# First input tile of a two-block transformer kernel on unnormalised x, with the token scale put on at eviction

## What is computed

```python
u = rms_norm(h, attn_pre_norm[i])          # x * rsqrt(mean(x*x) + 1e-6) * gain, per token
c_q, c_kv, k_rope, m_q, m_k, m_v, m_o, m_i, m_f = split_cols(u @ w_in[i], IN_SIZES)
q = (rms_norm(c_q, q_norm[i]) @ w_uq[i])
kv = (rms_norm(c_kv, kv_norm[i]) @ w_ukv[i])
```

## Time and profile before

| what | value |
|---|---|
| time, median of 3 runs | 1800.66 us (1800.34 to 1800.88) |
| the profiled execution | 1801.43 us, span 1799.6 us |
| TensorE busy | 1786.2 us (99%), 8494 matmuls |
| VectorE busy | 1396.1 us (78%) |
| ScalarE busy | 698.4 us (39%) |
| GpSimd busy | 1101.1 us (61%) |
| granted TensorE clock, mean | 0.999 |
| chain that ended last | PE 78%, DVE 1% |

### The profile page before, as it was taken

One profiled execution on the slowest core, in us unless ns is written; L12 is line 12 of the kernel. 1 busy time (PEld: TensorE's weight loads), 2 busy tenths in 40 slices (PEclk: granted clock), 3 DMA queues, 4 the chain that ended last, 5 costly groups with the idle time before them and its releaser, 6 DMA issues.

```text
span 1799.6 us, 22557 instructions
## 1 busy us (share of the span) xinstructions
PE 1786.2 (99%) x8494; PEld 1496.8 (83%) x8494; DVE 1396.1 (78%) x1617; ACT 698.4 (39%) x1219; POOL 1101.1 (61%) x772
## 2 busy tenths in 40 slices
PE   9999999999999999999999999999999999999998
PEld 9888888888888888888888888888888888888886
DVE  7889866656696758676599989579888875798897
ACT  6555577843431111111233334416433343333314
POOL 4066632260299979888778778632755565567554
PEclk9999999999999999999999999999999999999999
DMA  7342410032313323233375631113232231943222
GB/s 210 95 154 56 131 29 17 18 129 94 119 34 106 119 80 117 90 121 118 105 280 178 232 129 48 48 47 140 94 120 103 106 140 71 365 172 109 73 100 94
DMA packets 126975, 206.54 MB, mean 115 GB/s; under 512 B 32130, under 2 KB 88066, under 8 KB 123154
## 3 DMA queue, kind: packets, MB, share of 16 engines
q1 hardware_dynamic: 126690, 205.03, 33.4%
q10 hardware_dynamic: 176, 0.07, 0.0%
HBM read 151.51 MB, written 53.04 MB: 114 GB/s over the span
## 4 chain that ended last, share of the span: by engine, by line
PE 78%; DVE 1%; ACT 0%; issue 0%; DVEq 0%
PE ps L1382 68%; PE ps L1736 2%; PE ps L1738 2%; PE ps L1737 2%; PE ps L1982 1%; PE ps L1980 1%; PE ps L1981 1%; PE ps L1857 0%; PE ps L1883 0%; PE ps L1637 0%; PE ps L1723 0%; DVE ln_dev L3567 0%; PE ps L1610 0%; DVE y L3574 0%; DVE y L3726 0%; PE ps L1627 0%
## 5 line engine op out<-in xcount | busy, mean ns | idle before, releaser
L1382 PE MATMUL ps<-f_hi,ring_hi 128*128 128x512 f32 x368 | 143.4, 390 | 0.0
L1382 PE MATMUL ps<-f_hi,ring_lo 128*128 128x512 f32 x368 | 143.2, 389 | 0.0
L1382 PE MATMUL ps<-f_lo,ring_hi 128*128 128x512 f32 x368 | 143.2, 389 | 0.0
L1227 POOL TENSOR_TENSOR ring_lo<-w_sum,ring_hi 128x512 fp32r<-128x512 f32 x84 | 128.0, 1524 | 7.0
L1316 POOL TENSOR_TENSOR ring_lo<-w_sum,ring_hi 128x512 fp32r<-128x512 f32 x60 | 95.1, 1596 | 49.4 <-ACT ring_hi L2560 49.3
L2430 ACT ACTIVATE f_copy<-ps 128x512 f32<-128x512 f32 x63 | 37.4, 596 | 220.3 <-PE ps L1382 212.5
L1382 PE MATMUL ps<-d_w_hi,d_hid_hi 128*128 128x512 f32 x312 | 121.4, 389 | 0.0
L1382 PE MATMUL ps<-d_w_lo,d_hid_hi 128*128 128x512 f32 x312 | 121.4, 389 | 0.0
L1382 PE MATMUL ps<-d_w_hi,d_hid_lo 128*128 128x512 f32 x312 | 121.4, 389 | 0.0
L1382 PE MATMUL ps<-f_low,ring_hi 128*128 128x512 f32 x336 | 117.1, 389 | 0.0
L1382 PE MATMUL ps<-xs_hi,ring_hi 128*128 128x512 f32 x256 | 99.8, 390 | 0.0
(11 more groups left out here) (565 smaller groups left out, 5856.1 us busy)
## 6 DMA issues: line engine op xcount, KB each, us to landing
d_raw<-hid_rows SPq DMA_DIRECT2D x37, 512.0 KB, 4.9
stage<-in_w_up SPq DMA_DIRECT2D x22, 512.0 KB, 4.7
wd_raw<-in_w_down SPq DMA_DIRECT2D x22, 512.0 KB, 5.4
raw_w<-in_w_gate SPq DMA_DIRECT2D x20, 512.0 KB, 5.0
stage<-in_pool_w_in SPq DMA_DIRECT2D x16, 512.0 KB, 4.8
raw_w<-in_pool_w_in SPq DMA_DIRECT2D x16, 512.0 KB, 4.7
m_rows<-u_row SPq DMA_DIRECT2D x16, 512.0 KB, 2.6
z_rows<-z_buf SPq DMA_DIRECT2D x8, 1024.0 KB, 4.1
```

Source lines behind the costliest of these rows:

```text
L1227: g.tensor_tensor(view(lo), src, view(hi).bitcast(F32), ALU.subtract).then_inc(w_split, 1)
L1382: last = mm(out_ap, l, r, start=(start and j == 0), stop=(stop and j == n - 1), skip_group_check=onto)
```

## The change

Quarters 0 and 1 no longer go through rows and transposes. All four quarters of x are loaded by channel (`x_first` for quarter 0, `x_t` for 1 to 3), quarter 0 and 1 first, and go into `u_hi` and `u_lo` with the gain alone, without the token's scale. The first tile's product for tokens 0 to 511 is then multiplied by the token scale when it leaves PSUM, on VectorE. The scale is a row `r_first`, spread over all partitions by two matmuls (`first_spread`) in the second tile. After that quarters 0 and 1 are made again, with the scale, for all later work (`renorm`, `renorm_rounded`, `renorm_low`); the second tile does tokens 512 to 1023 first and waits part by part for the others. The x rows are still loaded for the statistics, those of quarters 0 and 1 last. Half of the row squares move from ScalarE to VectorE (`row_square` for 5, 7, 1, 3). GpSimd applies the gain to quarters 1 and 2, VectorE to quarter 3. Squares of `c_q` and `c_kv` and the parts `sq_hi` move from VectorE to ScalarE. The second weight tile is loaded before x rows 0 to 3 and the positions. Seven warm-ups are added at the start and the six behind the transposes are gone.

```diff
@@ sp_program
             src, view = zip(*(cols_tile(w_in, 0)(h) for h in range(2)))
-            for t in range(2):
-                x_rows(t)
+            def x_quarter(q, k, n):
+                c = KD + (KD * q + k) * QT
+                sp.dma_start(x_cols(q, k, n), a["x_t"][:, c:c + n * QT]).then_inc(x_in[q][k // 4], 16)
...
             for h in range(2):
                 sp.dma_start(view[h], src[h]).then_inc(staged[h], 16)
-            for t in range(2, 4):
-                x_rows(t)
+                x_quarter(0, 4 * h, 4)
+            for h in range(2):
+                x_quarter(1, 4 * h, 4)
             for q in range(2, 4):
...
+                x_row_pair(q)
+                x_quarter(q, 0, KD)
+            for h in range(2):
+                sp.wait_ge(parted[h], 1)
...
+            for q in range(2):
+                x_row_pair(q)
...
             load(V_TILE, value_tile(0))
-            sp.wait_ge(early_dve, 2)
-            sp.wait_ge(early_act, 2)
+            sp.wait_ge(early_dve, 4)
+            sp.wait_ge(early_act, 3)
@@ pe_program
+            def in_tile(s, bank0):
+
+                tile_ready(1)
+                for n in (1, 0):
+                    ts = slice(n * HALF, n * HALF + HALF)
+                    for m in range(2):
+                        for k in range(KD):
+                            if n == 0 and m == 0 and k % 2 == 0:
+                                pe.wait_ge(rows_split, 2 * TB + k + 2)
+                            if n and m == 0 and k == 2:
+                                first_spread()
...
-            for _ in range(15):
+            for _ in range(22):
                 mm(ps[:, 0, 0:P], ones[:], ones[:], start=True, stop=True)
             pe.wait_ge(consts, N_CONSTS)
-            x_transposed(0)
-            x_transposed(1)
-            for _ in range(6):
-                mm(ps[:, 0, 0:P], ones[:], ones[:], start=True, stop=True)
...
-            in_quarter(1, 2)
-            in_quarter(2, 4)
+            in_quarter(1, 5)
+            in_quarter(2, 5)
             in_quarter(3)
-            in_tile(1, 1, 4, 4, first=True)
+            in_tile(1, 4)
...
                     if r == 0:
-                        pe.wait_ge(in_taken, 4 + t + 1)
+                        pe.wait_ge(in_taken, (7, 7, 8, 8)[t] if t < 4 else 4 + t + 1)
@@ act_program
             value_weights_hi(0)
+            act.wait_ge(early_dve, 3)
+            for m in range(2):
+                act.wait_ge(in_taken, 4)
+                f(sq[:, m, :], c_q_raw[:, m, :], ACT.Square).then_inc(sq_made, 1)
...
             value_weights_hi(1)
+            act.wait_ge(early_dve, 5)
+            act.wait_ge(in_taken, 8)
+            f(sq[:, 1, :], c_kv_raw[:], ACT.Square).then_inc(sq_made, 1)
+            act.wait_ge(pos_in, POS_LANDED)
+            f(sq_hi[:, 0, :], sq[:, 0, :], ACT.Copy).then_inc(sq_made, 1)
+            act.wait_ge(sq_made, 3)
+            f(sq_hi[:, 1, :], sq[:, 1, :], ACT.Copy).then_inc(sq_made, 1)
@@ dve_program
+            first_low()
             dve.wait_ge(pool_hi.sem, 2)
             w0 = slice(1024, 2048)
             v.tensor_tensor(w_lo[0][:, w0], stage[:, 1, :], w_hi[0][:, w0].bitcast(F32), ALU.subtract).then_inc(parted[1], 1)
+            second_low(0)
+            row_square(5)
+            second_low(1)
             dve.wait_ge(consts, N_CONSTS)
             spread_row(4)
+            second_low(2)
+            second_low(3)
             spread_row(5)
...
+            u_pair(2, 0)
+            u_pair(2, 1)
+            u_pair_low(2, 0)
+            row_square(7)
+            u_pair(2, 2)
+            u_pair_low(2, 1)
+            u_pair(2, 3)
+            u_pair_low(2, 2)
+            u_pair_low(2, 3)
+            spread_row(6)
+            spread_row(7)
             u_quarter(3)
...
+            row_square(1)
+            row_square(3)
+            for t in range(4):
+                spread_row(t)
...
+            dve.wait_ge(early_act, 1)
+            renorm(0)
+            for j in range(4):
+                if j < 3:
+                    renorm(j + 1)
+                renorm_low(j)
+            dve.wait_ge(in_full, 2)
+            for m in range(2):
+                v.tensor_tensor(c_q_raw[:, m, 0:HALF], ps[:, m, :], r_first[:], ALU.mult).then_inc(early_dve, 1)
...
-            dve.wait_ge(in_taken, 4)
-            for m in range(2):
-                own.do(dve, v.tensor_tensor(sq[:, m, :], c_q_raw[:, m, :], c_q_raw[:, m, :], ALU.mult))
-            own.do(dve, v.tensor_tensor(sq[:, 0, :], sq[:, 0, :], sq[:, 1, :], ALU.add))
-            dve.wait_ge(in_taken, 6)
-            own.mark(v.tensor_tensor(sq[:, 1, :], c_kv_raw[:], c_kv_raw[:], ALU.mult))
-            dve.wait_ge(pos_in, POS_LANDED)
+            dve.wait_ge(sq_made, 2)
+            v.tensor_tensor(sq[:, 0, :], sq[:, 0, :], sq[:, 1, :], ALU.add).then_inc(early_dve, 1)
+            value_weights_lo(1)
             sq_split(0)
-            own.wait(dve)
             sq_split(1)
-            value_weights_lo(1)
```

More of the change, by code:

```diff
@@ L1403, in in_tile @@
-            def in_tile(t, s, q0, bank0, first=False):
-                tile_ready(t)
-                for m in range(2):
[L1406 to L1410, removed]
+            def in_tile(s, bank0):
[8 more added lines that the diff above has]
+                                first_spread()
+                            if n == 0 and m == 1 and k == 0:
+                                pe.wait_ge(early_act, 1)
+                            last = three(ps[:, bank0 + 2 * m + n, :], [(*wcols(s, k, m), u_hi[:, k, ts], u_lo[:, k, ts])],
+                                         start=(k == 0), stop=(k == KD - 1))
+                        last.then_inc(in_full, 1)
@@ L1425, in spread_columns, with first_spread @@
                 if q == 3:
-                    pe.wait_ge(rows_full, 12)
+                    pe.wait_ge(rows_full, 4)
                 cs = slice((q - 2) * QUARTER, (q - 1) * QUARTER)
                 mm(ps[:, SPREAD_BANK, 0:QUARTER], ones[:], spread[:, cs], start=True, stop=True).then_inc(gain_spread, 1)
+            def first_spread():
+                pe.wait_ge(rows_ready, TB)
+                pe.wait_ge(rows_split, 2 * TB)
+                for q in range(2):
+                    cs = slice((q + 2) * QUARTER, (q + 3) * QUARTER)
+                    mm(ps[:, FIRST_BANK, q * QUARTER:(q + 1) * QUARTER], ones[:], spread[:, cs], start=True, stop=True).then_inc(gain_spread, 1)
@@ new lines, in first_rounded, with second_rounded @@
+            def first_rounded():
+                for k in range(KD):
+                    if k % 4 == 0:
+                        act.wait_ge(x_in[0][k // 4], 16)
+                    ins = f(u_hi[:, k, 0:QT], x_cols(0, k), ACT.Copy, scale=gain_cols[:, k:k + 1])
+                    if k % 2:
+                        ins.then_inc(rows_hi, 1)
+            def second_rounded(pairs):
+                for j in pairs:
+                    act.wait_ge(pool_rows_ready, 2 * j + 2)
+                    f(u_hi[:, 2 * j:2 * j + 2, QT:2 * QT], pair_of(1, j), ACT.Copy).then_inc(rows_hi, 1)
@@ L2126, in value_row @@
                 if t == 0:
[L2127 removed]
+                    act.wait_ge(early_dve, 8)
                 if t >= 3:
@@ L2756, in spread_row, with row_square @@
-            def spread_row(t):
-                dve.wait_ge(row_sd, t + 1)
-                own.do(dve, v.reciprocal(stat_c[:, t:t + 1], stat_b[:, t:t + 1]))
-                v.tensor_scalar(spread[:, (t - 4) * P:(t - 3) * P], ident[:], stat_c[:, t:t + 1], None,
+            def row_square(t):
+                if DVE_ROWS.index(t):
+                    dve.wait_ge(kpe_split, DVE_ROWS.index(t))
+                dve.wait_ge(rows_in[t], 16)
+                v.scalar_tensor_tensor(junk1[:], x_nat[:, t, :], 1.0, x_nat[:, t, :], ALU.mult, ALU.mult,
+                                       accum_out=stat_a[:, t:t + 1]).then_inc(kpe_split, 1)
```

246 lines of the change are left out of this document (124 added, 122 removed).

## The result

The changed kernel takes 1821.24 us (median of four runs, 1821.06 to 1822.84), the kernel before 1800.5 (1799.99 to 1800.88): 1.0115 times as long, 95% interval 1.0103 to 1.0128, or 20.7 us more. The forecast was 1814.7 with a range up to 1820: the sign and the place are right, the size is 6.5 us short, and the time lies 1.2 us above the range. The profiled execution took 1821.31 us, its span is 1819.5 (1799.6 before).

The account below looks back on a forecast made before the run. TensorE's own work bounds the kernel (busy 1786.2 of 1799.6 us). Statistics starting 11.6 us later, early gains already spent, plus 2.4 for the clock gave +14.0: 1814.7 us, own range 1812.5 to 1817, outer ends 1809.5 and 1820.

Parts of the forecast that it names:

- Part 1: Start to quarter 1: first terms at 8.8, transposes gone, quarter 1 at about 14.6 instead of 19.25, a 4.7 us gain.
- not held: First quarter: TensorE needs 0.48 us a block, VectorE follows at 0.40, so TensorE would not wait.
- Part 2: Quarters 1 to 3: statistics work in VectorE's queue idles TensorE; quarter 3 ends at 36.1, leaving 1.6 of 4.7 us.
- if GpSimd works beside it, some 3: VectorE's row squares in quarters 1 to 3: 1.2 us each, or some 3 beside GpSimd; 1.2 was taken.
- a slower clock: Wait before the statistics: half-pace loss taken as 2.4 us, bounds 0 and 3.6; the longer slow stretch enters the upper end.
- late gate rows: Rival behind the statistics: gate rows come too late as well, 3 to 4 us more, 1818.2; chance 0.14.
- Part 3: Second tile: VectorE's angle block to 41.0, renorm and pairs to 51.5; tile ends at 59.0 against 59.51, gain 0.5 us.
- Part 4: VectorE behind the second tile: cos_q at 61.1, late copies and value tile; TensorE waits 10.8 us, statistics 11.6 us later.
- The clock: Behind the 10.8 us wait before the statistics: TensorE restarts at half pace and loses 2.4 us.
- The rival in which it doesn't fall: Wait before the statistics: the clock stays up, so +11.6 only, 1812.3 us; chance 0.12.
- After that: Gate rows onward: all engines shifted alike, 3.5 us VectorE idle as cover, cost nothing, up to 4 us without it.

Follow-up runs that it names:

- the late part: Changed kernel with cos_q early, statistics chain earlier, last split ahead of sums, second value weights ahead of u_rows(3), two sums and a split behind gate rows: 1808.3 us.
- the early one: Changed kernel with the first w_lo moved from GpSimd to VectorE behind its first group, and squares 5 and 7 back on ScalarE: 1818.22 us.
- the two runs with the chain moved: Changed kernel with cos_q, sum of squares, sq_hi and sq_lo earlier in their queues: 1816.81 us; with u_sum_lo(3) ahead of iq_sums(1) as well: 1814.47 us.
- the last run: Changed kernel with all early and late reorderings, plus row squares 6 and 7 earlier on ScalarE and first value-weight split ahead of two sums: 1805.17 us.

## Why the prediction was right in kind and short in size

The path was right: late `cos_q`, copies, load, ScalarE, statistics. What failed is the price of VectorE's passes in parts 1 and 2, eight passes at 3.2 us and a scaling at next to nothing: beside GpSimd they took 7.0 and 1.8 us. With what TensorE lost behind them `cos_q` came 5.3 us later than summed, of 5.9 us that the span is longer than forecast.

**Part 1.** The first real matmul was forecast at 8.8 and came at 8.15, since the 44 warm-ups took 7.22 us; ScalarE's blocks took 0.43 us instead of 0.38. The step that failed is "VectorE follows at 0.40 (8 in 3.22 us)", ending at 11.1: it ended at 14.1. The row was taken from another form of pass. It had GpSimd's two-operand pass beside it, and none of its passes was longer for that:
```profile
10.13 2.39 POOL L1119 TENSOR_TENSOR w_lo<-stage,w_hi 128x1024 fp32r<-128x1024 f32 x1
```
```profile
L2752 DVE SCALAR_TENSOR_TENSOR u_lo<-ps,x_t,u_hi x16: 473/476/484, 10.3 to 21.1; 128x256 fp32r<-128x256 f32 x16
```
Those passes read x out of PSUM (`ps`) and only `u_hi` out of SBUF; the new ones read `x_first` and `u_hi`, both out of SBUF. Beside GpSimd's two-operand pass they are 7.02, of which 2.57 us are a single pass; with that pass held off they are 4.24. TensorE, "not held" by the prediction, waited 2.39 us there and then lost some 1.6 at half pace up to 15.4, so quarter 1 started at 18.11 instead of 14.6.

**Part 2.** The bound "if GpSimd works beside it, some 3" for the row squares was in the text, taken from the earlier trace rows, and then the value without GpSimd was chosen, 1.2, "since GpSimd is mostly on one-operand passes then". They took 1.21 and 1.65 here, but the second took 2.95 in the profile of the run with the early `cos_q`; and the one-operand passes are no shelter, as the 1.30 us pass above shows. The 128-wide scaling, which stood still as well, was put at next to nothing. Quarter 3's first pair started at 33.65 instead of 28.0: 5.6 us, the largest miss of the sum. Of these 3.6 were there before it (quarter 2's spread at 22.43 for 18.8), 1.5 are the scaling and 0.5 the square. Nor did the bound find its way into the range, which took in only a slower clock and late gate rows (by its own terms its ends are 1809.8 and 1819.4, not 1809.5 and 1820).

**Part 3 and the length of VectorE's queue.** From quarter 3's first pair to `cos_q`, 33.1 us were summed and 32.7 measured. The work by the earlier trace rows was sized right; only its start was wrong. So `cos_q` came at 66.4, not at 61.1.

**Part 4.** From `cos_q` to the statistics 20.9 us were summed and 21.8 measured, nearly in the steps as told: 10.7 of SyncE's issue (10.5), landing at 81.4 (4.3 behind the start of the load's issue), ScalarE's five passes, and then both `sq_lo`, where one was summed behind ScalarE's last. TensorE's wait was 11.4 (10.8); it comes so close because both its ends were late, the start at 76.7 for 71.2 and the end at 88.1 for 82.0. The statistics started 17.7 us late (11.6): 5.3 by VectorE's start and 0.9 by the chain.

**The clock.** Forecast 2.4 us, measured 2.8: the statistics are at +17.7 (+17.75), the first block of another form behind them at +20.6 (125.51 against 104.92), with no wait between. The rival in which it doesn't fall is out. By the Trainium skill, TensorE: Matmul & The Clock Gate, Part 1, the engine starts throttled after idleness and activity releases it; now a row in the middle of the kernel agrees (granted clock 0.50 from 88 to 93.9). But the term isn't a cause that can be taken away by itself: with the wait filled, the same time was spent waiting for `iq_copy`, and the clock fell behind that wait instead.

**After that.** "I cost this at nothing; it costs up to 4 us if the cover is gone." The cover, 3.5 us of VectorE's idle time, was none: it lies in ScalarE's exp and log, which move along, and VectorE's own next step, the split at 111.88, was just in time before. In the changed kernel it hides, since TensorE was as late (a wait of 0.4). With the clock or the chain repaired it shows as 3.0 and 3.1 us, with `cos_q` late in the kernel before as 4.0. The end: 17.75 + 2.84 + 0.3 is 20.9 us at 137; 1.0 of it is given back further on, which the prediction had excluded ("nothing later gives time back"; the waits after 80 us are six lines, not seven), and the span is 19.9 longer.

**Where the 20.7 us come from, by the runs.** Of the 16.3 us that other places in the queues, and for three passes another engine, give back, 12.9 are the late part and 3.3 the early one (3.0 alone). The early part is the lateness of VectorE and TensorE together: no run here tells how much of it is GpSimd's passes, how much the squares and how much the clock at the start. The remaining 4.0 us (1804.98 against 1800.97 for the kernel before, timed with it) fell to no reordering tried here. VectorE has 13.0 us more work in the changed kernel by the page, and with the order repaired no gap over 0.3 us in its queue from 30.7 to 79 us, which agrees with that work as their cause; taking it away wasn't tried, so that is argued, not shown.

## What to carry to other kernels

When an edit puts work into a queue whose consumers are all a few us early, look for the one small result in that queue that another queue waits for: here three short passes (`cos_q`) release 10.7 us of DMA issue and a load behind it, and moving them alone costs 13.6 us. Price a VectorE pass by a row of the same form, above all with its operands in the same memory, and with the same neighbour on GpSimd: here the row read PSUM and the new pass SBUF, and 3.22 us became 7.02 beside the same kind of pass. If the trace has a cheap and a dear row, let the range reach to the dear one. A wait that is filled or removed pays only up to the next meeting point: read its slack from the start of the release to the start of what it releases, not from idle time elsewhere on the engine.

## What the runs showed of the hardware

Some of VectorE's passes don't just run slower beside a two-operand pass of GpSimd; they stand still until it ends. The 128-wide scaling of one SBUF operand (0.29 us alone) took 1.83 and 2.33 us, begun 0.61 and 0.13 us into GpSimd's pass and ended 0.08 us behind it in both cases; one of the first 256-wide passes, with both operands in SBUF, took 2.57 us, from 0.11 us behind the start of GpSimd's pass to 0.29 behind its end. Beside a one-operand pass of GpSimd such a pass took 1.30 us. The passes with one operand in PSUM weren't touched: 0.47 to 0.48 us each beside GpSimd's pass in the kernel before. The other side can wait as well: GpSimd's pass at 25.70, begun while VectorE's square was under way, took 3.22 us instead of 2.36. By the Trainium skill, SBUF — State Buffer, "SBUF: two separate sides", the two engines share a port pair that one of them locks for a whole instruction while the other blocks; these rows agree.

The granted clock fell to half in or behind waits of 11.39, 5.90, 4.63, 4.04 and 2.97 us, and behind the one of 2.39 us at the start, where it was 0.54 from 12 to 14. Shorter waits go either way: 0.50 behind one of 2.76 us and 1.00 behind one of 2.77 (the two runs with the chain moved), 0.50 behind one of 1.73 (GpSimd's pass held) and 1.00 behind one of 1.75 (squares on ScalarE). Behind the wait of 1.24 us in the last run the matmuls of 512 columns stayed 0.23 us apart.
